# The opening of a one-layer transformer kernel: smaller first modulation groups and another order of the first products

## What is computed

```python
mod = jax.nn.silu(c) @ w_ada[l] + b_ada[l]                       # w_ada is 1024 x 6144
sh1, sc1, gt1, sh2, sc2, gt2 = [m[:, None, :] for m in jnp.split(mod, N_MOD, axis=-1)]
h = rms_norm(x, g_norm_mix[l]) * (1.0 + sc1) + sh1
proj = h @ w_in[l]
...                                                              # two token mixers, merge, w_out
h2 = rms_norm(x, g_norm_ffn[l]) * (1.0 + sc2) + sh2              # then a gated feed-forward part
```

## Time and profile before

| | |
|---|---|
| median of 3 runs | 944.54 us (943.98 to 944.56) |
| the profiled execution, its time | 944.68 us |
| its span, first to last instruction | 943.0 us |
| TensorE busy | 913.0 us, 97% of the span |
| VectorE, ScalarE, GpSimd busy | 46%, 39%, 47% |

### The profile page before, as it was taken

One profiled execution on the slowest core, in us unless ns is written; L12 is line 12 of the kernel. 1 busy time (PEld: TensorE's weight loads), 2 busy tenths in 40 slices (PEclk: granted clock), 3 DMA queues, 4 the chain that ended last, 5 costly groups with the idle time before them and its releaser, 6 DMA issues.

```text
span 943.0 us, 11770 instructions
## 1 busy us (share of the span) xinstructions
PE 913.0 (97%) x4487; PEld 770.1 (82%) x4487; DVE 437.9 (46%) x707; ACT 363.7 (39%) x482; POOL 441.8 (47%) x390
## 2 busy tenths in 40 slices
PE   2999999999999999999999999999999999999996
PEld 1788898988978888888888888888888888888885
DVE  3843468683538978975714526322222222200005
ACT  5433335242443233353332337554445444412113
POOL 2579335253424433444543545455444455444554
PEclk9999999999999999999999999999999999999999
DMA  9842221212252858244525221422233222232212
GB/s 313 271 134 90 90 90 45 90 45 90 78 190 90 264 167 279 94 139 161 181 103 201 90 89 46 134 89 89 89 100 118 93 89 89 90 133 90 90 44 90
DMA packets 93767, 114.47 MB, mean 121 GB/s; under 512 B 2158, under 2 KB 84250, under 8 KB 93726
## 3 DMA queue, kind: packets, MB, share of 16 engines
q1 hardware_dynamic: 93726, 113.89, 36.5%
HBM read 111.76 MB, written 2.12 MB: 121 GB/s over the span
## 4 chain that ended last, share of the span: by engine, by line
PE 45%; issue 30%; POOL 20%; DVE 4%; ACT 1%; DMA 1%; POOLq 0%; SPq 0%; DVEq 0%; ACTq 0%
PE bank L1052 44%; POOL w_lo L656 19%; DVE bank L1515 1%; DMA x_in<-in_x_dram 1%; DVE bank L2015 0%; DVE x L2016 0%; PE bank L1055 0%; DVE xn_ffn L1906 0%; ACT h_tmp L762 0%; POOL masks L593 0%; ACT w_hi L735 0%; POOL masks L630 0%; DVE h_tmp2a L1571 0%; DVE part L1517 0%; DVE bank L1513 0%
## 5 line engine op out<-in xcount | busy, mean ns | idle before, releaser
L656 POOL TENSOR_TENSOR w_lo<-w_raw,w_hi 128x512 fp32r<-128x512 f32 x292 | 389.9, 1366 | 447.2 <-ACT w_hi L735 442.2
L1052 PE MATMUL bank<-h_hi,w_hi 128*128 128x512 f32 (+1 forms) x880 | 340.5, 390 | 0.1
L1052 PE MATMUL bank<-h_lo,w_hi 128*128 128x512 f32 (+1 forms) x880 | 337.2, 386 | 0.0
L1052 PE MATMUL bank<-h_hi,w_lo 128*128 128x512 f32 (+1 forms) x880 | 261.5, 386 | 0.0
L735 ACT ACTIVATE w_hi<-w_raw 128x2048 fp32r<-128x2048 f32 x72 | 137.5, 1910 | 223.4 <-PE bank L1052 223.4
L1052 PEld LDWEIGHTS bank<-h_hi,w_lo 128*128 128x128 f32 x880 | 165.6, 188 | 33.1
L1052 PEld LDWEIGHTS bank<-h_lo,w_hi 128*128 128x128 f32 x880 | 165.7, 188 | 32.7
L1052 PEld LDWEIGHTS bank<-h_hi,w_hi 128*128 128x128 f32 x880 | 165.4, 188 | 33.0 <-POOL h_lo L643 0.3
L1052 PE MATMUL bank<-w_hi,act_lo 128*128 128x512 f32 x176 | 68.5, 389 | 0.0
L1052 PE MATMUL bank<-w_hi,act_hi 128*128 128x512 f32 x176 | 68.5, 389 | 0.0
L1052 PE MATMUL bank<-w_lo,act_hi 128*128 128x512 f32 x176 | 68.5, 389 | 0.0
(11 more groups left out here) (250 smaller groups left out, 1119.4 us busy)
## 6 DMA issues: line engine op xcount, KB each, us to landing
w_raw<-in_w_in_dram SPq DMA_DIRECT2D x32, 1024.0 KB, 5.2
w_raw<-in_w_up_dram SPq DMA_DIRECT2D x22, 1024.0 KB, 5.1
ada<-in_w_ada_dram SPq DMA_DIRECT2D x16, 1024.0 KB, 5.3
w_raw<-in_w_down_dram SPq DMA_DIRECT2D x11, 1024.0 KB, 4.8
ada<-in_w_ada_dram SPq DMA_DIRECT2D x16, 512.0 KB, 8.6
w_raw<-in_w_out_dram SPq DMA_DIRECT2D x4, 1024.0 KB, 5.0
x_in<-in_x_dram SPq DMA_DIRECT2D x4, 512.0 KB, 5.3
w_raw<-in_w_in_dram SPq DMA_DIRECT2D x8, 256.0 KB, 7.2
```

The lines of the kernel that those rows point to most:

```text
L656: ins = pool.tensor_tensor(wlo[slot][:, cols], raw[slot][:, cols], whi[slot][:, cols].bitcast(F32), ALU.subtract)
L1052: return pe.matmul(o, lhsT, rhs, start=start, stop=stop, **kw)
```

## The change

- w_ada's first columns are summed in five groups instead of four: block 0 alone, block 1 alone (256 columns each), then the pairs (2,3), (4,5), (6,7). Their DMAs are cut into quarters of two row blocks: 16 DMAs of 128 KB in rows of 512 bytes for blocks 0 and 1, and 24 of 256 KB in rows of 1 KB, where there were 16 of 512 KB.
- The first weight shares stand ahead of block 1's columns in the DMA queue. The seven small loads of bias and gain rows are issued by ACT at its very start and no longer by SP.
- The inverse roots are made one token tile at a time; DVE scales tiles 0 and 1 of x, ACT tiles 2 and 3. TensorE transposes blocks 0 and 1 tile by tile.
- DVE makes the first two sums of the next group ahead of each `modulated`; the block's `h_lo(0)` moves from DVE to POOL.
- TensorE's products go over both units for a block's high part first, then the transposes, then the low part of h, then the next `first_modulation`, then the low part of the weights. Arithmetic and number of matmuls stay; each modulation of a single block takes two of its one-column matmuls instead of four.
- POOL makes `h_lo` ahead of `w_lo` in each round; ACT makes the high parts of a weight share ahead of h.

```diff
+MOD_GROUPS = ((0,), (1,), (2, 3), (4, 5), (6, 7))
...
-            for half in range(2):
-                ada_half(0, half)
-            rows(vec_rows, B_ADA, b_ada.rearrange("l (k p) -> (l k) p", p=P), 48)
...
-            first_shares(0)
-            for half in range(2):
-                ada_half(1, half)
-            for j in range(2, KT // 2):
-                ada_half(j, 0)
-                first_shares(j - 1)
-                ada_half(j, 1)
-            first_shares(KT // 2 - 1)
-            ready(sp, ("mod1", 1))
+            for g in range(len(MOD_GROUPS)):
+                for q in range(4):
+                    ada_quarter(g, q)
+                if g != 1:
+                    first_shares(max(g - 1, 0))
+            ready(sp, ("mod1", 2))
...
-            pool.wait_ge(sq_done, TT)
-            inverse_root(0, TT)
+            for t in range(TT):
+                pool.wait_ge(sq_done, t + 1)
+                link(pool.tensor_scalar(rstd[:, t:t + 1], ssq[:, t:t + 1], 1.0 / D, EPS, ALU.mult, ALU.add))
+                pool.tensor_tensor(rstd[:, t:t + 1], rstd[:, t:t + 1], mhalf[:, 0:1], ALU.pow).then_inc(first_root, 1)
...
             for j in range(KT // 2):
+                if j < KT // 2 - 1:
+                    low_h(2 * j)
+                    if j:
+                        low_h(2 * j + 1)
                 low_share(j, 0)
                 low_share(j, 1)
-                if 0 < j < KT // 2 - 1:
-                    low_h(2 * j)
-                if j < KT // 2 - 1:
-                    low_h(2 * j + 1)
+                if j == 0:
+                    low_h(1)
...
             for j in range(KT // 2):
-                act.wait_ge(share_in[j], 16 * 2)
                 high_share(j, 0)
+                if j == 0:
+                    first_h(0)
                 high_share(j, 1)
-                first_h(j)
+                if j:
+                    first_h(2 * j)
+                first_h(2 * j + 1)
...
+            high, h_low, w_low = (whi, h_hi), (whi, h_lo), (wlo, h_hi)
+            first_transposes()
+            vector_rows()
+            first_modulation(0)
+            for u in range(2):
+                growing_products(u, 0, *high)
+            first_modulation(1)
...
+            first_modulation(2)
+            for g in (2, 3):
+                for k in MOD_GROUPS[g]:
+                    for u in range(2):
+                        growing_products(u, k, *high)
+                for k in MOD_GROUPS[g + 1]:
+                    transposed_x(k)
+                for k in MOD_GROUPS[g]:
+                    for u in range(2):
+                        growing_products(u, k, *h_low)
+                first_modulation(g + 1)
+                for u in range(2):
+                    for k in MOD_GROUPS[g]:
+                        growing_products(u, k, *w_low)
+            for u in range(2):
+                for what in (high, h_low, w_low):
+                    for k in MOD_GROUPS[-1]:
+                        growing_products(u, k, *what)
...
+            for t in range(2):
+                scaled_x(t)
+            group_sums(0, range(KT))
...
+            for g in range(1, len(MOD_GROUPS)):
+                group_sums(g, range(2))
+                modulated(g - 1)
+                group_sums(g, range(2, KT))
+            modulated(len(MOD_GROUPS) - 1)
```

More of the change, by code:

```diff
@@ L120, in plan_banks @@
         use(("xT", 0, k), "start")
-    for j in range(KT // 2):
-        use(("mod1", j), "mod1")
+    for g in range(len(MOD_GROUPS)):
+        use(("mod1", g), "mod1")
     for u, t, pool in ((0, 0, "gemm"), (0, 1, "gemm"), (1, 0, "gemm"), (1, 1, "fourth")):
@@ L345, in layer_kernel @@
         hi_done = sem("hi_done")
-        share_in = [sem(f"share_in{j}") for j in range(KT // 2)]
+        share_in = [[sem(f"share_in{j}_{u}") for u in range(2)] for j in range(KT // 2)]
         hi_share, lo_share = sem("hi_share"), sem("lo_share")
@@ L353, in layer_kernel @@
         c_in, vec_in = sem("c_in"), sem("vec_in")
-        ada_in = [[sem(f"ada_in{j}_{half}") for half in range(2)] for j in range(KT // 2)]
+        ada_in = [[sem(f"ada_in{g}_{q}") for q in range(4)] for g in range(len(MOD_GROUPS))]
+        first_root = sem("first_root")
         pair_done = sem("ada_pair_summed")
@@ L370, in layer_kernel @@
         rstd_done = sem("rstd_done")
-        xn_done = [sem("xn_act"), sem("xn_dve")]
+        xn_done = [sem(f"xn_done{t}") for t in range(TT)]
         xn2_done = [sem(f"xn_ffn_tile{t}") for t in range(TT)]
@@ L1351, in small @@
                     filled(ins, ("mod2", u - 1))
-            def growing_products(j, u):
-                if j < KT // 2 - 1:
-                    pe.wait_ge(lo_share, 2 * j + u + 1)
-                else:
[L1358 to L1372, removed]
-                    pe.wait_ge(h_hi_done, k + 1)
-                    both_tiles(k, parts[0], h_hi, False)
-                    both_tiles(k, parts[1], h_hi, False)
-                    pe.wait_ge(h_lo_done[k], 1)
-                    both_tiles(k, parts[0], h_lo, k == KT - 1)
@@ L1518, in pair_sums @@
-                    if j == 1 and k == 1:
-                        low_h(0)
-                    if j > 1 and k == 1:
-                        modulated(j - 1)
-            def modulated(j):
-                b = ready(dve, ("mod1", j))
-                cols, scales = slice(2 * j, 2 * j + 2), slice(KT + 2 * j, KT + 2 * j + 2)
-                tt(mod[:, cols], b[:, 0:2], vec[:, B_ADA + 2 * j:B_ADA + 2 * j + 2], ALU.add)
-                release(tt(mod[:, scales], b[:, 2:4], vec[:, B_ADA + KT + 2 * j:B_ADA + KT + 2 * j + 2], ALU.add), ("mod1", j))
-                evacuated(dve, ("mod1", j))
-                stt(a1[:, cols], mod[:, scales], 1.0, vec[:, G_MIX + 2 * j:G_MIX + 2 * j + 2], ALU.add,
+                        stt(part[:, g % 2, 0:n], src, sc, acc, ALU.mult, ALU.add).then_inc(pair_done, 1)
@@ new lines, in modulated @@
+            def modulated(g):
+                b = ready(dve, ("mod1", g))
+                k0, n = MOD_GROUPS[g][0], len(MOD_GROUPS[g])
+                cols, scales = slice(k0, k0 + n), slice(KT + k0, KT + k0 + n)
+                tt(mod[:, cols], b[:, 0:n], vec[:, B_ADA + k0:B_ADA + k0 + n], ALU.add)
+                release(tt(mod[:, scales], b[:, n:2 * n], vec[:, B_ADA + KT + k0:B_ADA + KT + k0 + n], ALU.add), ("mod1", g))
+                evacuated(dve, ("mod1", g))
+                stt(a1[:, cols], mod[:, scales], 1.0, vec[:, G_MIX + k0:G_MIX + k0 + n], ALU.add,
```

193 lines of the change are left out of this document (110 added, 83 removed).

## The result

The changed kernel takes 947.6 us (median of 6 runs, 947.43 to 948.68) against 944.45 of before on the same chip (6 runs, 943.49 to 944.56). The ratio is 1.0037, 95% interval 1.0026 to 1.0048: slower by about 0.4%, or 3 us, where 944.9 was forecast, and outside the forecast's range too. The profiled executions are 944.68 before and 948.55 after.

What follows compares the result with a forecast made beforehand. TensorE, busy 913.0 of 943.0 us, was taken as the bound. M at 29.0 plus 25.3 puts unit 2 at 54.3, 0.4 us later: 945.0, less 0.14 for the median, gives 944.9 us; range 943.3 to 946.9.

Steps and rivals of the forecast that it cites:

- The loop: Opening, from M to unit 2: two rounds of 7.99 us, then 4.22 and 22 products (5.08), M + 25.3 us.
- M: TensorE's modulation of pair (2,3) in the opening, forecast at 29.0 us, set by TensorE and not by DVE's 27.7.
- first round: TensorE from M to the next modulation, first of two equal rounds: 4.22 us to h_hi, products and transposes, 7.99 us.
- last modulation to unit 2: End of the opening: 4.22 us to the second h_hi, then 22 products in 5.08 us.
- unit 2: Start of the third unit's products, from where units follow without a gap: forecast at 54.3 us instead of 53.91.
- The waits: TensorE idle ahead of h_hi products: some 2 us behind M, 0.4 to 0.9 us ahead of each second block.
- a rival in which the clock is low: Clock stays at 1.2 GHz up to M, so M at 32.1 and 948.0 us; chance 14%.
- `a1` behind GpSimd: DVE's a1 for block 1 held by GpSimd until 22.9 us; h_hi(1) at 24.35 instead of 24.0, TensorE not ready for either.
- The start: Opening up to M: block 0 alone lets the first product start at 18.9 us, 6.0 us ahead of before.
- Small DMAs at nothing: Loads of blocks 0 and 1 in 512-byte rows: landing 0.6 and 1.3 us later, costing nothing.
- the timetable: DMA landings in the opening: data number B (in MB) is there at 18.02 + (B - 4.72) / 0.348 us.
- The start carries through: Rival: gapless TensorE stream from 18.9 us ends 6 us sooner, 938.7; half of that, 941.7, more likely; chance 6%.

Runs made afterwards that it cites:

- e8: Changed kernel plus eight products of zeros behind the modulation of pair (2,3), and GpSimd's w_lo ahead of h_lo for shares 1 to 3: 944.77 us.
- e1: Changed kernel plus eight products of zeros on TensorE filling the wait behind the modulation of pair (2,3): 946.58 us.
- e3: Changed kernel with GpSimd making w_lo ahead of h_lo again for shares 1 to 3: 946.45 us.
- e4: Changed kernel with each modulation from pair (2,3) on moved ahead of the products with h_lo on TensorE: 943.09 us.
- e7: Changed kernel with TensorE's order of before and GpSimd's w_lo first (in share 0, only unit 0's ahead of h_lo(0)): 943.19 us.
- e9: Changed kernel with only the modulation of pair (2,3) moved ahead of block 1's eight h_lo and w_lo products, later rounds unchanged: 946.8 us.
- e6: Changed kernel with TensorE's order of before, GpSimd's new order kept: 950.73 us.

## Why the prediction was wrong

The step that failed is the one under *The loop*: "Two rounds, then 4.22 and 22 products (5.08): M + 25.3 us". It measured M + 29.4. By its parts:

| | forecast | changed kernel | e8 |
|---|---|---|---|
| M | 29.0 | 28.43 | 28.43 |
| first round | 7.99 | 9.18 | 8.13 |
| second round | 7.99 | 8.11 | 8.09 |
| last modulation to unit 2 | 9.30 | 12.12 | 9.40 |
| unit 2 | 54.3 | 57.84 | 54.05 |

- *The waits.* Foreseen: 2.05 us behind M ("some 2 us"), 0.60 ahead of the second block ("0.4 to 0.9"); the 1.17 ahead of block 6 is the late `a1` of the next point. What they set off was not foreseen. The sum counts the products behind a wait at 0.231 us each; it took 2.4 GHz as kept once reached. Eight of them took 3.61 us. The first fall costs 1.05 us (9.18 against 8.13), the second 1.6: the products from 51.69 to unit 2 take 6.15 us, the same ones in e1 4.56 (51.28 to 55.84). The profiles without either fall (e8, and e1 in the last stretch) have the products at the forecast's pace. The prediction had a rival in which the clock is low, and placed it ahead of M, where it did rise in time. Its 948.0 us is close to the result for another reason, so it doesn't count as right.
- *`a1` behind GpSimd.* The prediction described this block from the earlier trace rows and applied it to block 1, where it changes nothing. It used the 0.42 and 4.22 us of before for the later modulations without asking what the new order of GpSimd does there. It is 1.29 us instead of 0.16 and goes in full into the last stretch (2.72 us over e8, of which 1.13 this and 1.59 the fall). e3 shows it: 0.16 us, and no wait ahead of block 6's products. The Trainium skill, SBUF — State Buffer, Who interferes with whom, says that a VectorE instruction with two inputs in SBUF contends with a GpSimd instruction that reads SBUF, over ports that only one of them can hold. The trace agrees: `a1` ends within 0.01 us of the end of a single `w_lo`, the fourth of the run in the changed kernel (48.25) and the second in e4 (43.37).
- *The start.* The first product at 18.97 (18.9), block 0's sums by 14.97 (15.4), steps of 256 columns in PSUM at 0.52 us (0.52), M at 28.43 (29.0), DVE's part of it at 27.37 (27.7). Right, and M was TensorE's as said: its one-column matmuls at 28.43 have no wait. The half us between forecast and profile says little, as M stood at 29.04 when the same kernel ran once more: there the clock rose later, and block 0's four products with `w_lo` took 1.91 us instead of 1.58.
- *Small DMAs at nothing.* Right in the result. The landings of w_ada were about 0.7 us later than the timetable (27.73 us for one that it has at 27.04), and M came early nevertheless; in e8 the rounds and the last stretch come within 0.3 us of the sum without them.
- *The start carries through* was given 6% at 941.7 us. e4 (943.1, 1.1 us under its before) and e7 (943.2, 1.3 us under) put it at little more than 1 us of the 6, with no wait over 0.8 us behind a modulation.

What stays open: why the same waits are followed by a fall in some executions and not in others. The waits of 1.18 and 0.60 us had one in both profiles of the changed kernel, none in those of e1 and e9. e4's waits (1.17, one-column matmuls and eight products, 0.76) had none either. That the first fall costs its 1.1 us is shown by the product times and by e1, which takes it away. The second was never taken away by an edit of its own: its 1.6 us rest on the product times of executions with and without it. What exactly brings a fall on isn't shown.

## What to carry to other kernels

When a reorder opens holes in TensorE's stream, cost each hole twice: its length, and the work behind it at half the clock until it rises again; in the changed kernel the fall behind a hole of 2.05 us cost a further 1.1 us, and the one behind two holes of 1.17 and 0.60 us a further 1.6, in some executions and not in others. Put the modulation (or whatever another engine must answer) ahead of independent products that last as long as the answer takes: that edit alone, e4, is worth 4.5 us here. Before you reorder one engine, list what it will ask of the others and when: TensorE's old order is the slowest run with GpSimd's new order (e6, 950.7) and level with the best with a fitting one (e7, 943.2), while the changed kernel gains when GpSimd takes back its old order for shares 1 to 3 (e3, 946.5). And look in the new order for a small VectorE operation that now meets a run of GpSimd's.

## What the runs showed of the hardware

- The granted clock fell to 0.50 (1.2 GHz) after TensorE had gone through eight one-column matmuls and a wait of 2.05 us, and again after eight products, a wait of 1.17, two products and one of 0.60. It stayed there 3.4 to 3.5 us in the changed kernel and 6.8 us in e6, there from 1.5 us behind a wait of 2.12 us.
- Whether it falls behind the same waits of 1.18 and 0.60 us differs between executions: it did in the changed kernel's two profiles and didn't in those of e1 and e9. Within one kernel this is only suggested, by e9's times. The moment of the rise does differ within one kernel: block 0's four products with `w_lo` took 1.58 us in one profile of the changed kernel and 1.91 in the other. The Trainium skill, TensorE: Matmul & The Clock Gate, What's actually happening, states that the gate's count isn't aligned with the kernel's start and that the moment of the transition so varies; the two profiles agree as to the moment, and no run here shows the cause.
- A VectorE operation of 128x2 with both inputs in SBUF that takes 0.16 us alone took 1.29, 0.82 and 0.36 us beside GpSimd's `w_lo` operations of 1.28 us each, and ended with one of them: it is held for the rest of one operation, not for a run of four.
- The windows that hold the transfers of 128 KB in rows of 512 bytes, queued with others, ran at 311 to 326 GB/s, those with 256 KB in rows of 1 KB at 349.
